# Two stages of a token model on one core: state space chunks with three passes on GpSimd and a norm per chunk; the time mix recurrence joined with its output stage

## The reference

```python
def mamba2_branch(z, xbc, dt_raw, ...):
    ...
    y = ssd_chunked(xs, dt, a, bm, cm)               # two chunks of 128 tokens
    y = y + xs * d_skip[:, None]
    y = y.reshape(b, s, SSD_D_INNER) * jax.nn.silu(z)
    yg = y.reshape(b, s, SSD_GROUPS, SSD_D_INNER // SSD_GROUPS)
    yg = yg * lax.rsqrt(jnp.mean(yg * yg, -1, keepdims=True) + SSD_NORM_EPS)
    return yg.reshape(b, s, SSD_D_INNER) * norm_w

def rwkv7_time_mix(h, ...):
    ...
    g = jax.nn.sigmoid(xg @ g1) @ g2                 # (256, 160) @ (160, 1024)
    def step(state, inp):
        r_t, d_t, k_t, v_t, kk_t, a_t = inp
        sa = jnp.einsum('bhij,bhj->bhi', state, -kk_t)
        state = (state * d_t[:, :, None, :] + sa[..., None] * (kk_t * a_t)[:, :, None, :]
                 + v_t[..., None] * k_t[:, :, None, :])
        return state, jnp.einsum('bhij,bhj->bhi', state, r_t)
    ...
    mean = jnp.mean(y, -1, keepdims=True)
    var = jnp.mean(jnp.square(y - mean), -1, keepdims=True)
    y = ((y - mean) * lax.rsqrt(var + RWKV_GN_EPS)).reshape(b, s, d)
    y = y * ln_g + ln_b
    bonus = jnp.sum(r_ * k_ * r_k, -1, keepdims=True) * v_
    y = y + bonus.reshape(b, s, d)
    return (y * g) @ w_o
```

## Time and profile before

| | us |
|---|---|
| median of 3 runs (1957.23 to 1958.78) | 1957.58 |
| the profiled execution | 1958.1 |
| its span | 1956.3 |
| PE busy | 1758.5 (90% of the span) |
| DVE busy | 1105.6 |
| ACT busy | 655.7 |
| POOL busy | 10.4 |

### The profile page before, as it was taken

The page is one execution under the profiler, slowest core; times in us unless marked ns, Lnnn a source line. Parts: engine busy times, 40 slices in busy tenths (PEclk is TensorE's granted clock), DMA queues, the critical chain, the costliest instruction groups (busy, mean ns, idle before and its releaser), DMA issues. The chain is left out here.

```text
span 1956.3 us, 30051 instructions
## 1 busy us (share of the span) xinstructions
PE 1758.5 (90%) x12670; PEld 1304.8 (67%) x12670; DVE 1105.6 (57%) x1993; ACT 655.7 (34%) x1037; POOL 10.4 (1%) x6
## 2 busy tenths in 40 slices
PE   6898789988988899999987999999998988769998
PEld 5343256763323588888875788878886876558887
DVE  4332254452322777773578677677777372658665
ACT  3111013331100644442243544464444302045443
POOL 0000000000000000000000000000000000200000
PEclk9898889989987999999978999999999989779999
DMA  8999972279999755434211455545542312045540
GB/s 357 415 421 421 421 293 80 93 298 420 421 421 421 296 194 193 162 104 183 105 47 58 157 178 188 183 162 189 180 168 84 131 38 89 4 150 189 182 168 22
DMA packets 58190, 405.27 MB, mean 207 GB/s; under 512 B 6416, under 2 KB 7824, under 8 KB 10432
## 3 DMA queue, kind: packets, MB, share of 16 engines
q1 hardware_dynamic: 58048, 403.25, 53.5%
HBM read 402.18 MB, written 1.05 MB: 206 GB/s over the span
## 5 line engine op out<-in xcount | busy, mean ns | idle before, releaser
L2092 PE MATMUL ps<-ffn_x,ffn_wh 128*128 128x512 f32 x1408 | 496.2, 407 | 10.4 <-DVE ffn_x L2226 7.2
L2095 PE MATMUL ps<-ffn_x,ffn_wl 128*128 128x256 f32 x1408 | 376.6, 281 | 0.0
L2092 PEld LDWEIGHTS ps<-ffn_x,ffn_wh 128*128 128x128 f32 x1408 | 269.6, 192 | 84.1 <-issue 11.0
L2233 DVE TENSOR_TENSOR ffn_wl<-w,ffn_wh 128x2048 fp32r<-128x2048 f32 x132 | 301.4, 2286 | 1.7 <-ACT ffn_wh L2177 0.3
L2095 PEld LDWEIGHTS ps<-ffn_x,ffn_wl 128*128 128x128 f32 x1408 | 258.2, 189 | 1.6
L2177 ACT CAST ffn_wh<-w 128x2048 fp32r<-128x2048 f32 (+1 forms) x140 | 252.9, 1806 | 4.5 <-PEq L715 3.5
L2192 ACT COPY ffn_part_low<-ps 128x512 f32<-128x512 f32 x88 | 51.5, 585 | 338.7 <-PE ps L2095 337.9
L2237 DVE TENSOR_TENSOR ffn_z<-ps,ffn_part_low 128x512 f32<-128x512 f32 x88 | 60.8, 690 | 161.2 <-ACT ffn_part_low L2192 161.0
L2136 PE MATMUL ps<-ffn_wh,ffn_hidh 128*128 128x512 f32 x352 | 138.2, 393 | 0.4 <-issue 0.4
L2138 PE MATMUL ps<-ffn_wh,ffn_hidl 128*128 128x512 f32 x352 | 137.5, 391 | 0.0
L2137 PE MATMUL ps<-ffn_wl,ffn_hidh 128*128 128x512 f32 x352 | 137.3, 390 | 0.0
(11 more groups left out here) (588 smaller groups left out, 2722.0 us busy)
## 6 DMA issues: line engine op xcount, KB each, us to landing
w<-in_ffn_gu SPq DMA_DIRECT2D x88, 1024.0 KB, 4.8
w<-in_moe_gu SPq DMA_DIRECT2D x70, 1024.0 KB, 18.6
w_extra<-in_moe_gu SPq DMA_DIRECT2D x52, 1024.0 KB, 25.9
w<-in_ffn_dn SPq DMA_DIRECT2D x44, 1024.0 KB, 4.8
w_extra<-in_moe_dn SPq DMA_DIRECT2D x32, 1024.0 KB, 26.2
w<-in_moe_dn SPq DMA_DIRECT2D x26, 1024.0 KB, 26.8
sq<-in_moe_dn SPq DMA_DIRECT2D x6, 1024.0 KB, 27.9
sq<-in_moe_gu SPq DMA_DIRECT2D x6, 1024.0 KB, 26.5
```

Source lines behind the costliest of these rows:

```text
L2092: return nc.tensor.matmul(pair_of(b)[:, a], high[:, s, tile(a, k)], X[:, k], start=k == 0, stop=False)
L2095: return nc.tensor.matmul(pair_of(b)[:, a, 0:SEQ], low[:, s, tile(a, k)], XH[:, k], start=False, stop=k == KT - 1)
L2233: nc.vector.tensor_tensor(low[:, s], S.buf(units[n]), high[:, s], ALU.subtract).then_inc(*w_split.one())
```

## The change

In the state space stage, `xdd` and both skips go to GpSimd, the copy of the state goes to ACT (behind the exponent of unit 3), and the norm is taken chunk by chunk: squares, Sqrt, reciprocal and scalings of chunk 0, then of chunk 1.

In the time mix, `rwkv_output` is gone. The bonus and `ln_b` move into `rwkv_inverse`, on GpSimd. The making of `Sd` goes from DVE to GpSimd. In chunk `c` DVE also sums the `y` of chunk `c - 1` (`total`) and centres that of chunk `c - 2` (`centre`), and ACT makes the squares of chunk `c - 1` (`spread`). Behind the loop DVE does the four remaining passes in two halves and four pairs, and PE makes the gate. The gate's PSUM columns are now 256 to 511 of each bank, and its two products follow each other for each `q`. The cut diff:

```diff
@@ ssd_chunks
             def states():
-                pe.wait_ge(*st_in.at(1))
+                pe.wait_ge(*st_in.at(2))
...
-            link(act, K.act_step, squares(0))
-            link(act, K.act_step, squares(1))
-            nc.scalar.activation(ms[:, :, :, 1:2], ms[:, :, :, 0:1], ACT.Sqrt, ...).then_inc(*rooted.one())
+                if u == 3:
+                    act.wait_ge(*st_made.at(1))
+                    for g in range(SSD_GROUPS):
+                        last = nc.scalar.copy(state[:, g], K.ps[:, 6 + g])
+                    last.then_inc(*st_taken.one())
+            for c in range(2):
+                link(act, K.act_step, squares(c))
+                nc.scalar.activation(ms[:, c, :, 1:2], ms[:, c, :, 0:1], ACT.Sqrt, ...).then_inc(*rooted.one())
+
+        @block.gpsimd
+        def _(pool):
+            def skip(c):
+                nc.gpsimd.tensor_tensor(hp(xs[:, c]), hp(xs[:, c]), heads(row[:, 2]), ALU.mult).then_inc(*skipped.one())
+            pool.wait_ge(*xd_made.at(1))
+            pool.wait_ge(*e_done.at(1))
+            nc.gpsimd.tensor_tensor(hp(xdd[:]), hp(xd[:, 0]), heads(acs[:, 0, 1]), ALU.mult).then_inc(*st_in.one())
+            skip(0)
+            pool.wait_ge(*xd_made.at(2))
+            skip(1)
...
-            dve.wait_ge(*rooted.at(1))
-            do(v.reciprocal(ms[:, :, :, 0:1], ms[:, :, :, 1:2]))
             for c in range(2):
+                dve.wait_ge(*rooted.at(c + 1))
+                do(v.reciprocal(ms[:, c, :, 0:1], ms[:, c, :, 1:2]))
@@ rwkv_chunks: PE
+            def gate(c):
+                tok = slice(c * RC, (c + 1) * RC)
+                for q in range(4):
+                    R, cols = quad(q), slice(q * QW, (q + 1) * QW)
+                    nc.tensor.matmul(K.ps[R, (c + 4) % 8, QW:2 * QW], low[:, 0, tok], S_.buf(ga)[:, cols], start=True, stop=False, tile_position=(0, q * RC))
+                    mm = nc.tensor.matmul(K.ps[R, (c + 4) % 8, QW:2 * QW], low[0:GATE_LORA - P, 1, tok], S_.buf(gb)[:, cols], start=False, stop=True,
+                                          tile_position=(0, q * RC))
+                if c % 2:
+                    mm.then_inc(*g_made.one())
...
+            for c in range(N_RC):
+                if c == 4:
+                    pe.wait_ge(*y_done.at(N_RC))
+                gate(c)
@@ rwkv_chunks: GpSimd
+            for c in range(1, N_RC - 1):
+                pool.wait_ge(*st_ready.at(c))
+                link(pool, carried, nc.gpsimd.tensor_tensor(Sd[:], S[:], cl[:, :, c:c + 1].to_broadcast([P, KT, HD]), ALU.mult))
+                nc.gpsimd.tensor_tensor(Sd[:], Sd[:], kv[c], ALU.add).then_inc(*carried.one())
@@ rwkv_chunks: DVE, behind the loop
+            for i, part in enumerate(halves):
+                n = N_RC // 2
+                dve.wait_ge(*rooted.at(i + 1))
+                link(dve, K.dve_step, vv.reciprocal(st[:, 4, part], st[:, 3, part]))
+                for c in (N_RC - 2, N_RC - 1) if i else ():
+                    centre(c)
...
+                link(dve, K.dve_step, vv.tensor_tensor(at, at, by, ALU.mult))
+                link(dve, scaled, vv.tensor_tensor(y[:, part], y[:, part], ln[:, 0:1].to_broadcast([P, n, QW]), ALU.mult))
+                link(dve, K.dve_step, vv.tensor_tensor(y[:, part], y[:, part], g[:, part], ALU.add))
+            for p in range(4):
+                dve.wait_ge(*g_made.at(p + 1))
+                pair, banks = slice(2 * p, 2 * p + 2), slice((2 * p + 4) % 8, (2 * p + 4) % 8 + 2)
+                vv.tensor_tensor(y[:, pair], y[:, pair], K.ps[:, banks, QW:2 * QW], ALU.mult)
```

More of the change, by code:

```diff
@@ L3123, in _ @@
             relative(3)
-            skip(0)
             weigh(3)
             relative(4)
-            dve.wait_ge(*st_made.at(1))
-            v.tensor_copy(state[:], K.ps[:, 6:8].rearrange("p g n -> p g n")).then_inc(*st_taken.one())
             weigh(4)
             relative(5)
-            dve.wait_ge(*xd_made.at(2))
-            skip(1)
             weigh(5)
@@ L3445, in rwkv_inverse @@
             S.free(wv[j], v_unit.at(j + 1) if j < 3 else v_made.at(N_RC))
+        unit, bonus_made = S.take("ln_rows"), K.sig("scaled")
+        ln = S.buf(unit).rearrange("p (j n) -> p j n", j=2)
+        heads = lambda ap: ap.rearrange("p c (h d) -> p (c h) d", d=HD)
         tok = lambda c: slice(c * RC, (c + 1) * RC)
@@ L3632, in _, with spread, root @@
                 mm.then_inc(*y_made.one())
+            pe.wait_ge(*S_.arrived(ga))
+            pe.wait_ge(*S_.arrived(gb))
+            for c in range(N_RC):
+                if c == 4:
+                    pe.wait_ge(*y_done.at(N_RC))
+                gate(c)
         @block.scalar
         def _(act):
+            def spread(c):
+                act.wait_ge(*sum_made.at(c + 1))
+                link(act, K.act_step, nc.scalar.activation(st[:, 1, c], st[:, 0, c], ACT.Copy, scale=-1.0 / HD))
+                for h in range(4):
+                    last = nc.scalar.activation(junk[:], y[:, c, h * HD:(h + 1) * HD], ACT.Square, bias=st[:, 1, c, h], accum_out=st[:, 2, c, h])
+                    if h < 3:
+                        link(act, K.act_step, last)
+                last.then_inc(*spread_made.one())
+            def root(i):
+                act.wait_ge(*spread_made.at(N_RC // 2 * (i + 1)))
+                nc.scalar.activation(st[:, 3, halves[i]], st[:, 2, halves[i]], ACT.Sqrt, bias=K.eps[:, 2:3], scale=1.0 / HD).then_inc(*rooted.one())
             for c in range(N_RC):
@@ L3642, in _, with total, centre @@
             vv = nc.vector
+            def total(c):
+                dve.wait_ge(*y_done.at(c + 1))
+                vv.reduce_sum(st[:, 0, c], heads(y[:, c]), AX).then_inc(*sum_made.one())
+            def centre(c):
+                dve.wait_ge(*spread_made.at(c + 1))
+                at = heads(y[:, c])
+                vv.tensor_tensor(at, at, st[:, 1, c].to_broadcast([P, 4, HD]), ALU.add).then_inc(*centred.one())
             for c in range(N_RC):
@@ L3646, in _ @@
                     vv.tensor_tensor(of_g(W), of_par[:, :, :, 0], of_g(nv[0][:, c]), ALU.add).then_inc(*w_ready.one())
[L3647 to L3650 removed]
+                    total(c - 1)
                 dve.wait_ge(*sa_made.at(2 * c + 1))
                 vv.tensor_copy(SA[:, 0:P], K.ps[:, 2, 0:P]).then_inc(*sa_ready.one())
+                if c > 1:
+                    centre(c - 2)
                 if c:
```

147 lines of the change are left out of this document (54 added, 93 removed).

## The result

The changed kernel takes 1972.3 us (median of four executions: 1969.13, 1970.03, 1974.49 and 1998.66) against 1957.4 us for the kernel before (four executions). The ratio of the means is 1.0108, 95% interval 1.0075 to 1.0142; the long execution of 1998.66 is in it, and the medians alone stand 1.0076 apart. So it is slower, by 0.8 to 1.1%, and the median lies 1.4 us from the 1973.7 forecast. The profiled execution took 1969.13 us, its span is 1967.3.

The account below looks back on a forecast made before the run. No engine is full in the recurrence, a PE-DVE chain; DVE bounds the output stage, one chain the state space end. +16.8 - 2.7 + 2.0 = +16.1 on 1958.1 gives 1974.2, median 1973.7; range 1962 to 1992.

Parts of the forecast that it names:

- The gate on PE: Output stage: 64 matmuls of alternating kinds run one by one, 38.2 us; the next stage starts 16.8 us later.
- nothing of the next kind starts before the last pass is through: Gate on PE: a change of matmul kind waits for all running passes, so one matmul costs what a set did.
- the estimate of 1.0: Gate on PE: price of one alternating matmul at 1.2 GHz, 0.85 us plus 0.15 for the change of kind.
- The two parts of the 0.57: Gate on PE at 2.4 GHz: 0.46 us for a set without a change, plus 0.11 for the change of kind.
- The recurrence, -1.0: Recurrence chunks: with `Sd` off DVE, the gain is between 0 and 3 us, taken as 1.0.
- where the copy was late PE gains what it stood: Recurrence: PE gains about 0.4 us where it waited for DVE's late copy, counted in three of eight chunks.
- The end of the output stage: After PE's gate: one last multiplication with its start, 0.7 us, and the barrier, 0.3, before the next stage.
- State space stage: End -2.7 us from the moved table load and scalings by chunk; front +2.0 from GpSimd holding DVE's clamps.
- the rule that would have made the front +4: State space front: DVE instructions with two SBUF inputs and GpSimd ones reading SBUF exclude each other, holding each `weigh` too.
- DMAs, bonus and `ln_b` at nothing: DMAs freed some 20 us later by the gate, and bonus and `ln_b` on GpSimd in the inverse, cost nothing.
- The kinds don't exclude each other: Rival for the gate: different kinds run side by side, 14.7 us, total 1950 (0.12); at 1.2 GHz 27.3 us, 1963 (0.05).
- The clock stays low: Rival for the gate: the clock doesn't rise, 64 matmuls at 1.0 us each, total 1999.5; chance 0.08.

Follow-up runs that it names:

- the gate by sets: The changed kernel, but in each chunk four gate matmuls of 128 by 32, then four of 32 by 32: 1946.0 us (single execution).
- the one-kind kernel: The changed kernel with its order of places, but the gate's second product repeats the first's operands, so all 64 are 128 by 32: 1951.3 us (single execution).
- the second profiled execution: The changed kernel run again unchanged, for its spread and the clock: this profiled execution took 1967.98 us, the median of the six is 1971.3.

## Why the prediction was right

**The gate on PE.** Right in mechanism and size. 64 matmuls one by one, 35.0 us against 38.2 forecast: 0.547 each in place of 0.57, and all of them at 2.4 GHz in place of four at 1.2. The step "nothing of the next kind starts before the last pass is through" is what the gate by sets and the one-kind kernel confirm, and 0.99 for one matmul at 1.2 GHz meets the estimate of 1.0. The two parts of the 0.57 were off and cancelled: a set without a change takes 0.43 (the 3.7 us of the earlier trace rows hold the last pass running out besides the eight sets), and scaled to 272 columns that leaves 0.14, not 0.11, for the change. That the gate had the high clock from its first matmul is no merit of the reasoning: in the second profiled execution it began at the low one.

**The recurrence, -1.0.** Wrong: it gained nothing. From its first matmul to the start of its last product it took 34.7, 34.8, 35.6 and 36.2 us in four kernels with the old recurrence, 34.9 to 35.6 in nine executions with the new one. The failing step is "where the copy was late PE gains what it stood": the copy does come in time now (DVE mostly waits 0.25 to 0.45 us for PE there), but the period of a chunk stays at 4.5 to 4.9 us in most chunks. PE's wait for that copy, 1.4 us in three chunks before, is gone in every trace with the decay on GpSimd, and the length is not, so a late copy was not what set it. Nor was PE bound by its clock in the slow chunks, as the prediction had it: three executions with the whole recurrence at 0.50 took 34.9 to 35.4 us, as long as those partly at 1.00. What does set it stays open.

**The end of the output stage.** The next stage started 1.25 us after the last multiplication's start, forecast 1.0. Together: +1.0 for the recurrence, -3.2 for the gate, +0.3: the forecast 74.0 us from the recurrence's start became 72.2.

**State space stage.** End -2.6 (forecast -2.7), front +1.4 in the profiled execution and up to +2.1 in others, where the clock fell (forecast +2.0). The holds were 1.20, 0.25 and 0.98 us where I had 1.2, 0.6 and 1.2. The forecast counted the 1.0 us of the two skips twice, once against the copy and once against the holds; by its own terms it should have said +3.0. It came near because the second hold was shorter and the copy cost nothing beside GpSimd's passes, so part of that term was luck. No weighing was held by GpSimd, because none started during a pass, so the rule that would have made the front +4 did its work only on GpSimd's side.

**DMAs, bonus and `ln_b` at nothing.** From the next stage's start to the end of the program it is 236.0 us, before 237.0: the late release of the gate's two units costs nothing. Between the two stages four kernels with the bonus in the output stage took 602.8 to 604.8 us and ten with it in the inverse 603.3 to 606.2; a cost under 1 us there can't be told from the spread.

**The rivals.** "The kinds don't exclude each other" (1950, or 1963 at the low clock) fell with the traces. By the Trainium skill, TensorEngine Tiling (Array Packing), "Key Properties", different tiles run independently and a change of tiling mode drains; the traces agree with both, 0.43 us for four of one kind and 0.547 for one between two of the other. "The clock stays low" (0.08, 1999.5) was priced right and rated too low: three of ten executions took 1998.7 to 2003.1. My argument against it, that the clock is high for a third of the recurrence, says at best how often the gate begins at the high level. The clock did rise in an alternating gate once, 1.1 us after its start, and stayed low for 63 us in another kernel, and no row of before told which it would be. The median held because seven of the ten were short, which is luck. The chances don't add up either: the cases that make the kernel slower had 0.75, 0.05 and 0.08, which is 0.88, and the forecast says 0.84.

## What to carry over

When small matmuls share the array by column parts, keep those of one shape together, in whole sets at least: here a change of shape cost 0.14 us if it came once in four matmuls, and all that running side by side gives if it came at every one (0.547 us for one matmul, where four took 0.43). Before joining two stages, write down which engine the join leaves last, and check that the reordering has not changed how that one runs; here a correct move (8 us) was hidden under a loss of 23. A pass moved to GpSimd was no relief where DVE had clamps within SBUF beside it: DVE was held for the rest of the pass, so time such passes by what DVE does then, or leave them. And before two single executions are compared, look at the granted clock in the stretch: a difference of 1.4 us that seemed to belong to a copy belonged to the clock.

## What the runs showed that I had not expected

- Two matmuls behind each other in the same column part, accumulating in the same bank, cost nothing against two in different parts: 0.43 us for four either way, as long as the shape is the same. In the trace four firsts ran side by side, then four seconds.
- One kernel has two times, some 1970 and 2001 us. In the traces alternating stretches ran at 1.00 for 35 us, at 0.50 for 63 us, and at 0.50 for 1.1 us and then at 1.00. In the kernel before, dense sets ahead of it made the high level more likely: all four executions were long without them, two of ten with them.
- GpSimd's pass over 128x1024 took 1.90 us alone, 2.08 where it came up behind a held clamp, and 2.28 behind a weighing: each of the two engines waits for the other.
